# First modulation in five slabs, half of the value products in three one-pass products, scale and shift on ScalarE

## The reference, cut to what matters

```python
mod = cond @ w_ada[l] + b_ada[l]                       # cond = silu(c): one row times a 2048 x 6144 matrix
shift, scale, gate = jnp.split(mod, 3, axis=-1)
h = rms_norm(x, norm_g[l]) * (1.0 + scale[:, None, :]) + shift[:, None, :]
z = h @ w_in[l]
u_a, v_a, g_a, q_b, k_b, v_b, g_b, f_b = jnp.split(z, pts, axis=-1)
```

## Time and profile before

| | |
|---|---|
| median of 3 runs | 2876.5 us (2872.1 to 2881.73) |
| the profiled execution, its time | 2872.35 us |
| its span, first to last instruction | 2870.5 us |
| mean granted TensorE clock | 0.995 |
| busy: TensorE matmuls, VectorE, ScalarE, GpSimd | 2784.9, 1790.2, 1044.7, 43.1 us |
| value stage, first to last value product | 54.05 to about 170.7 us |
| f group, first to last product | 170.66 to about 182.05 us |
| DMA share and rate, 100 to 125 us | 1.00, 350 GB/s |

### The profile page before, as it was taken

The page is one execution under the profiler, slowest core; times in us unless marked ns, Lnnn a source line. Parts: engine busy times, 40 slices in busy tenths (PEclk is TensorE's granted clock), DMA queues, the critical chain, the costliest instruction groups (busy, mean ns, idle before and its releaser), DMA issues.

```text
span 2870.5 us, 35410 instructions
## 1 busy us (share of the span) xinstructions
PE 2784.9 (97%) x12484; PEld 2204.4 (77%) x12484; DVE 1790.2 (62%) x2750; ACT 1044.7 (36%) x1632; POOL 43.1 (2%) x51
## 2 busy tenths in 40 slices
PE   7999999999999989999999999999999999999999
PEld 4468887777788866888877777787778688888887
DVE  6856675555598768445565747383977777525454
ACT  3032222444332365422243534433322542224233
POOL 0000000000000000000000000000000000100000
PEclk9999999999999999999999999999999999999999
DMA  9966553222356647466522223224667265333332
GB/s 353 353 212 214 190 190 96 74 76 79 126 192 219 231 145 244 149 216 197 185 82 83 82 86 103 73 88 139 216 231 220 90 234 192 108 97 96 124 111 96
DMA packets 239243, 451.32 MB, mean 157 GB/s; under 512 B 23919, under 2 KB 45889, under 8 KB 234483
## 3 DMA queue, kind: packets, MB, share of 16 engines
q1 hardware_dynamic: 236288, 440.85, 46.8%
q0 software_dynamic: 2304, 8.39, 0.8%
q10 hardware_dynamic: 504, 0.17, 0.0%
HBM read 422.06 MB, written 27.30 MB: 157 GB/s over the span
## 4 chain that ended last, share of the span: by engine, by line
PE 85%; DVE 5%; ACT 2%; issue 2%; DVEq 2%; DMA 2%; ACTq 1%; SPq 1%
PE ps L1405 20%; PE ps L1411 20%; PE ps L1408 20%; PE ps L1695 4%; PE ps L1424 2%; PE ps L1418 2%; PE ps L1421 2%; PE ps L1936 2%; PE ps L1853 1%; PE ps L1844 1%; PE ps L1375 1%; PE ps L1970 1%; PE ps L1967 1%; PE ps L1380 1%; PE ps L1377 1%
## 5 line engine op out<-in xcount | busy, mean ns | idle before, releaser
L1993 DVE TENSOR_TENSOR w_lo<-w_raw,w_hi 128x512 fp32r<-128x512 f32 (+2 forms) x672 | 448.3, 673 | 542.2 <-ACT w_hi L714 297.8
L1405 PE MATMUL ps<-op_hi,w_hi 128*128 128x512 f32 (+2 forms) x2800 | 779.2, 397 | 6.5 <-ACT w_hi L714 4.5
L1411 PE MATMUL ps<-op_hi,w_lo 128*128 128x512 f32 (+2 forms) x2800 | 754.7, 389 | 5.2 <-DVE w_lo L1993 5.2
L1408 PE MATMUL ps<-op_lo,w_hi 128*128 128x512 f32 (+2 forms) x2800 | 754.9, 389 | 0.6 <-DVE op_lo L2130 0.6
L1411 PEld LDWEIGHTS ps<-op_hi,w_lo 128*128 128x128 f32 (+1 forms) x2800 | 524.8, 188 | 117.8 <-DVE w_lo L1993 7.1
L1408 PEld LDWEIGHTS ps<-op_lo,w_hi 128*128 128x128 f32 (+1 forms) x2800 | 526.1, 188 | 112.8 <-DVE op_lo L2130 1.4
L1405 PEld LDWEIGHTS ps<-op_hi,w_hi 128*128 128x128 f32 (+1 forms) x2800 | 517.4, 188 | 121.8 <-issue 10.3
L714 ACT ACTIVATE w_hi<-w_raw 128x512 fp32r<-128x512 f32 (+2 forms) x416 | 242.7, 592 | 596.0 <-PE ps L1411 437.2
L739 ACT ACTIVATE w_hi<-w_raw 128x512 fp32r<-128x512 f32 x288 | 181.8, 632 | 583.7 <-PE ps L1411 454.2
L2016 DVE SCALAR_TENSOR_TENSOR acc<-a_raw,vec,acc 128x512 f32<-128x512 f32 x525 | 382.1, 747 | 17.5 <-DMA a_raw<-in_w_ada 14.8
L2758 DVE TENSOR_TENSOR w_lo<-w_raw,w_hi 128x512 fp32r<-128x512 f32 x128 | 83.6, 686 | 60.7 <-ACT w_hi L1262 55.2
(11 more groups left out here) (314 smaller groups left out, 2459.3 us busy)
## 6 DMA issues: line engine op xcount, KB each, us to landing
a_raw<-in_w_ada SPq DMA_DIRECT2D x216, 512.0 KB, 4.0
w_raw<-in_w_in_e SPq DMA_DIRECT2D x160, 512.0 KB, 4.7
w_raw<-in_w_in SPq DMA_DIRECT2D x96, 512.0 KB, 4.8
arena<-in_w_ada SPq DMA_DIRECT2D x72, 512.0 KB, 6.7
w_raw<-in_w_in_o SPq DMA_DIRECT2D x64, 512.0 KB, 4.3
w_raw<-in_w_out SPq DMA_DIRECT2D x32, 512.0 KB, 4.9
w_raw<-in_w_out_e SPq DMA_DIRECT2D x32, 512.0 KB, 5.2
w_raw<-in_w_out_o SPq DMA_DIRECT2D x32, 512.0 KB, 3.8
```

The source lines that it names most:

```text
L1405: mm(ps[0:m, bank + j, 0:tok], hi[:, cols], B.op_hi[:, k, 0:tok], start=first, stop=False)
L1408: mm(ps[0:m, bank + j, 0:tok], hi[:, j * P:j * P + m], B.op_lo[:, k, 0:tok], start=False, stop=False)
L1411: last = mm(ps[0:m, bank + j, 0:tok], lo[:, j * P:j * P + m], B.op_hi[:, k, 0:tok], start=False, stop=last_t)
L1993: V.tensor_tensor(B.w_lo[:, c % RING, 0:width], B.w_raw[:, c // 2 % RAW, c % 2, 0:width], B.w_hi[:, c % RING, 0:width].bitcast(f32), ALU.s ...
```

## The change

- The first modulation is made in 5 slabs of 4, 4, 4, 2, 2 tiles. The last two have loads of 256 KB and accumulates of 128x512, 16 each; the norm is 128x1024, the sums are 4 products.
- Scale and shift move from VectorE to ScalarE (`ACT.Identity` with scale and bias). In slabs 0 and 1 the four tiles are modulated and then rounded. From slab 2 (`SPLIT_SLAB`) on ScalarE makes `op_hi` straight from the normed tile, drains, and then modulates the tile in place.
- The value products of slabs 2, 3 and 4 (blocks 8 to 15, 64 of the 128 products) become three fp32r products each. Their 16 weight tiles are split: `w_hi` by ScalarE (`value_high`; the first four ahead of slab 2, those of slabs 3 and 4 behind the slab's tiles), `w_lo` by GpSimd (`value_low`, one 128x512 `tensor_tensor` each), between its loads.
- In slabs 2 to 4 the order within a block is tile by tile; ahead of them, in blocks that are odd, stand the two tiles' products of bank 7. The sums of slabs 3 and 4 are placed behind these, so 18 one-pass products are behind the sums.
- VectorE has the low parts from accumulate 3 on, the norm ahead of park, and the last slab's low parts, its park and the first f weights' low parts between the 16 part accumulates.
- The store of x moves from SyncE's to ScalarE's queue, the load of b_s behind f's weights. The weights of f wait for `lo_done`. The two buffers of the slabs are exchanged.

```diff
-START_RING, SLABS, SLAB = 6, 4, 4
+START_RING, SLABS = 6, 5
+SLAB_AT, SLAB_TILES = (0, 4, 8, 12, 14), (4, 4, 4, 2, 2)
+SPLIT_SLAB = 2
...
+def value_low(B, pool, b):
+    for c in (2 * (b - SPLIT_BLOCK), 2 * (b - SPLIT_BLOCK) + 1):
+        pool.wait_ge(B.sem("hi_done"), c + 1)
+        if c >= RING:
+            pool.wait_ge(B.sem("w_used"), c - RING + 1)
+        B.nc.gpsimd.tensor_tensor(B.w_lo[:, c % RING, :], B.w_raw[:, b % RAW, c % 2, :],
+                                  B.w_hi[:, c % RING, :].bitcast(mybir.dt.float32), mybir.AluOpType.subtract)
+        B.nc.gpsimd.drain().then_inc(B.sem("lo_done"), 1)
...
+        if b >= SPLIT_BLOCK + RAW:
+            value_low(B, pool, b - RAW)
         pool.dma_start(B.w_raw[:, b % RAW, :, :],
...
     for slab in range(SLABS):
+        split = 2 * (SLAB_AT[slab] - SPLIT_BLOCK)
+        if slab == SPLIT_SLAB:
+            for c in range(RING):
+                value_high(c)
+        act.wait_ge(sem("columns_or_parked"), 2 * slab + 1)
+        for t in range(SLAB_TILES[slab]):
+            k = SLAB_AT[slab] + t
+            x, scale, bias = slab_input(B, slab)[:, t, :], B.mod[:, 16 + k:17 + k], B.mod[:, k:k + 1]
+            if slab >= SPLIT_SLAB:
+                Act(B.op_hi[:, k, :], x, ACT.Identity, scale=scale, bias=bias).then_inc(sem("op_high"), 1)
+                nc.scalar.drain()
+            Act(x, x, ACT.Identity, scale=scale, bias=bias).then_inc(sem("modulated"), 1)
+        if slab < SPLIT_SLAB:
...
+        else:
+            for c in range(max(split, RING), split + 2 * SLAB_TILES[slab]):
+                value_high(c)
...
+    def split_products(slab, b, k, blocks):
...
+        for j in blocks:
+            mm(bank, B.op_hi[:, t, rows(j)], hi, start=first, stop=False)
+        pe.wait_ge(sem("lo_done"), c + 1)
+        for j in blocks:
+            mm(value_bank(slab, g, t, j)[0], B.op_hi[:, t, rows(j)], lo, start=False, stop=False)
+        pe.wait_ge(sem("op_tile"), t + 1)
+        for j in blocks:
+            done = mm(bank, B.op_lo[:, t, rows(j)], hi, start=False, stop=last)
...
+                if b == final:
                     last.then_inc(sem("park_summed"), 1)
+                    if slab >= SPLIT_SLAB and slab < SLABS - 1:
+                        reduce_slab(slab + 1)
...
             if kt == 1:
                 slab_columns(slab - 1)
-                slab_modulated(slab - 1)
-            if kt in (4, 5, 6, 7):
-                slab_low(slab - 1, kt - 4)
+            if 3 <= kt < 3 + SLAB_TILES[slab - 1]:
+                slab_low(slab - 1, kt - 3)
             if kt == 15:
+                slab_normed(slab)
                 park(slab - 1)
-                slab_normed(slab)
     slab_columns(SLABS - 1)
-    slab_modulated(SLABS - 1)
-    for t in range(SLAB):
-        slab_low(SLABS - 1, t)
     for t in range(KT):
         part_tile(FIRST["f"], t)
-    park(SLABS - 1)
+        if t < SLAB_TILES[SLABS - 1]:
+            slab_low(SLABS - 1, t)
+        if t == 9:
+            park(SLABS - 1)
+        if t in (9, 11):
+            if t == 9:
+                dve.wait_ge(sem("lo_done"), KT)
+            low_tile(KT + (t - 9) // 2, GROUPS[FIRST["f"]]["width"])
```

More of the change, by code:

```diff
@@ L618, in pool_program @@
             .then_inc(B.va_in[b % RAW], 16)
+    for b in range(KT - RAW, KT):
+        value_low(B, pool, b)
     queries = at(AT_QST, 2, S)
@@ L1683, in reduce_slab @@
         if slab:
-            pe.wait_ge(sem("parked"), slab)
+            pe.wait_ge(sem("columns_or_parked"), 2 * slab)
         else:
             pe.wait_ge(sem("variance"), 1)
-        reduce_parts(slab % 2, ps[:, 7, :]).then_inc(sem("start_summed"), 1)
+        tiles = SLAB_TILES[slab]
+        for v in range(2):
+            for j in range(tiles):
+                last = mm(ps[:, 7, tiles * v + j:tiles * v + j + 1], B.acc[:, slab % 2, v, j * P:(j + 1) * P],
+                          B.ones[:, 0:1], start=True, stop=True)
@@ L1689, in value_product, with value_bank @@
+        last.then_inc(sem("start_summed"), 1)
+    def value_bank(slab, g, t, j):
+        own = g == 1 and j == 3
+        first, last = (SLAB_AT[slab], SLAB_AT[slab] + SLAB_TILES[slab] - 1) if own else (0, KT - 1)
+        return ps[:, 4 * g + j, :], t == first, t == last
     def value_product(slab, b, k, j):
-        g, kt = va_block(b)
+        g, kt = VA_BLOCKS[b]
+        t = kt + k
         pe.wait_ge(B.va_in[b % RAW], 16 * (b // RAW + 1))
-        t = kt + k
-        own = g == 1 and j == 3
@@ L1695, in value_product @@
-        return mm(ps[:, 4 * g + j, :], slab_input(B, slab)[:, t % SLAB, j * P:(j + 1) * P],
-                  B.w_raw[:, b % RAW, k, :], start=t % SLAB == 0 if own else t == 0,
-                  stop=t % SLAB == SLAB - 1 if own else t == KT - 1)
+        pe.wait_ge(sem("modulated"), t + 1)
+        bank, first, last = value_bank(slab, g, t, j)
+        return mm(bank, slab_input(B, slab)[:, t - SLAB_AT[slab], j * P:(j + 1) * P],
+                  B.w_raw[:, b % RAW, k, :], start=first, stop=last)
@@ new lines, in split_products @@
+    def split_products(slab, b, k, blocks):
+        g, kt = VA_BLOCKS[b]
+        t, c = kt + k, 2 * (b - SPLIT_BLOCK) + k
+        hi, lo = B.w_hi[:, c % RING, :], B.w_lo[:, c % RING, :]
+        rows = lambda j: slice(j * P, (j + 1) * P)
+        pe.wait_ge(sem("hi_done"), c + 1)
+        pe.wait_ge(sem("op_high"), t + 1)
+        for j in blocks:
+            bank, first, last = value_bank(slab, g, t, j)
+            mm(bank, B.op_hi[:, t, rows(j)], hi, start=first, stop=False)
[4 more added lines that the diff above has]
+        for j in blocks:
+            bank, first, last = value_bank(slab, g, t, j)
+            done = mm(bank, B.op_lo[:, t, rows(j)], hi, start=False, stop=last)
+        return done
@@ L2452, in slab_low @@
     def slab_low(slab, t):
-        k = SLAB * slab + t
+        k = SLAB_AT[slab] + t
         dve.wait_ge(sem("op_high"), k + 1)
@@ L2516, in vector_program @@
     y_tile = lambda t: Y[:, t, :]
-    for c in range(4):
+    for c in (KT + 2, KT + 3):
         low_tile(c, GROUPS[FIRST["f"]]["width"])
```

141 lines of the change are left out of this document (77 added, 64 removed).

## The result

| | before | after |
|---|---|---|
| median, us (executions) | 2874.86 (4) | 2903.89 (4) |
| lowest to highest | 2872.1 to 2881.73 | 2899.93 to 2908.33 |
| profiled execution / its span | 2872.35 / 2870.5 | 2903.88 / 2902.1 |
| mean granted clock in it | 0.995 | 0.987 |
| f's first product / q's first product, us | 170.66 / 184.02 | 192.12 / 208.07 |

The ratio is 1.0091 (95% interval 1.0077 to 1.0106). The two medians lie 29 us apart, more than twice what was forecast and outside its range; the ratio alone makes it 26 us. At q's first product the delay in the profiled executions is 24.05 us.

A forecast was written before the change was run, and what follows sets the result against it. TensorE was taken as the bound, barely, with VectorE close behind. VectorE's and GpSimd's delays gave +11 us at f's end, clock +1.7, queues +0.6: taken as +13 on 2876.5, so 2889.5 us; range 2869 to 2900.

The forecast's parts named there:

- The store of x takes a turn in ScalarE's queue (0.45 us), beside TensorE: Queue term: the moved store of x costs ScalarE's queue 0.45 us, beside TensorE's work.
- plus 0.15 to signal: Low weight tiles on GpSimd: signalling each finished subtraction adds 0.15 us to its 1.25.
- GpSimd's 1.25 us: Split value products: one 128x512 subtraction on GpSimd takes 1.25 us, a quarter of a longer instruction and a start.
- The exclusion, accumulates too: Slabs 2 to 4: each of 16 GpSimd subtractions takes 1.25 us from VectorE, holding its accumulates; bounds 0 and 1.25.
- TensorE's −10.7: Value products: if only TensorE counted, 64 split products save 11.6 us, less 0.9 for another set of sums.
- The wait of 8 us ahead of slab 4's sums: TensorE reaches slab 4's sums near 152.4 us, VectorE at 160.5, so TensorE waits 8 us.
- The clock, +1.7: Slow clock behind TensorE's gaps: hidden at 134 and 152 us, counted in the f group, +1.7 us.
- q keeps its distance to f's end: q group: its weights follow f's low tile 10, so its start shifts along with f's end.
- A: Rival: accumulates not held by GpSimd, value stage ends near 167.7 us, total 2874.5 us; chance 0.15.
- D: Rival: halved loads with 1 KB rows move fewer bytes, VectorE waits for loads, +3 us more; within chance 0.15 shared with C.
- C: Rival: GpSimd's subtractions take 1.5 to 1.9 us, adding 4 to some 10 us, 2893 to 2900; chance 0.15.
- B: Rival: TensorE stays the bound and the full -10.7 us returns, 2866 us, likelier end 2868; chance 0.05.

The follow-up runs named there:

- e_late: The changed kernel with the store of x moved on ScalarE's queue behind the evacuation of f's bank: 2894.69 us, ratio 1.0068 to the kernel before.
- e_late_nodrain: e_late with GpSimd's drain behind each subtraction removed, the subtraction signalling by itself: 2886.56 us, ratio 1.0035 to the kernel before.
- e_late_memset: e_late_nodrain with GpSimd's subtraction replaced by four memsets of 128x128: 2878.34 us, ratio 1.0007 to the kernel before.
- e_last_only: The changed kernel with late store, low weight parts on VectorE, slabs of 4, 4, 4, 4 tiles, only the last split: 2873.87 us, ratio 0.9991.
- e_last_again: The same kernel as e_last_only, run again in another set: 2873.92 us, ratio 0.9991 to the kernel before.
- e_whole: The changed kernel with late store, low weight parts on VectorE, slabs of 4, 4, 4, 4 tiles, the last two split: 2880.29 us, ratio 1.001.
- e_memset: The changed kernel with GpSimd's subtraction replaced by two memsets with a drain between: 2904.23 us (one execution).

## Why the prediction was wrong

The direction was right and the size was not: +13 forecast, +29 measured by the medians and +26 by the ratio. The delay of q's first product (24.05 us in the profiles) falls in three steps of known cause, which the experiments take away one behind the other:

| taken away | kernel | q's first product, less by | between the marks, less by | ratio, less by |
|---|---|---|---|---|
| the store's place | e_late | 7.2 us | 5.6 us | 0.0023 (6.6 us) |
| the drains | e_late_nodrain | 7.1 us | 7.0 us | 0.0033 (9.5 us) |
| GpSimd's reading beside VectorE | e_late_memset | 9.6 us | 11.5 us | 0.0028 (8.1 us) |

What is left is within 0.3 us of the kernel before at both marks, and 0.0007 by the ratio, whose interval takes in 1. The three views of a step differ by 1.6 to 3.4 us, which is how well its size is known. Only the third was in the sum.

- **The step that failed first** was "The store of x takes a turn in ScalarE's queue (0.45 us), beside TensorE". It costed the issue (0.36 us in the profile) and not the 4 MB behind it, while it did cost the bytes of b_s, an eighth as many. Nor did it ask when the store would now be issued: at 173.12 instead of 149.85. The landing of f's first weights became 9.9 us in the middle, and the Gelu that stands behind them on ScalarE kept TensorE from f for 8.17 us. With the store elsewhere this hole is gone, and the time is 6 to 9 us less.
- **The second** was GpSimd's "plus 0.15 to signal". The term was a drain behind a load in flight. Four of them took 4.0 to 5.6 us. "Waits some 2.5 us for the first low tiles" became 5.18, and slab 3's sums came at 144.1 instead of 139. Without the drains TensorE's waits for GpSimd fall from 7.0 to 1.6 us.
- **GpSimd's 1.25 us**: right, 1.27 at the shortest, up to 1.59 in the kernel after.
- **The exclusion, accumulates too**: right. e_late_nodrain is the kernel that the sum described. Its VectorE takes from columns (110.41) to the end of the park (136.92) 26.5 us; the sum had 16.3 + 8 x 1.25 = 26.3. Its f starts at 177.08, against 177.8 in the sum; TensorE waits there for VectorE's low tile until 181.33, with 183.2 in the sum; its last f product begins at 191.89, against an end of 193. This execution was ahead by 2 us already at slab 2's columns (110.41, against 112.4 in the sum); from there to f's end it takes 81.7 us, and the sum had 80.6. Its time is 9.3 us over the kernel before, where the sum said 13. The Trainium skill (SBUF — State Buffer, "SBUF: two separate sides") has this exclusion for VectorE instructions with two SBUF inputs beside a reading GpSimd; the runs agree: 1.34 us per accumulate over a stretch with subtractions beside it, 0.84 with memsets beside it.
- **TensorE's −10.7**: the rates were right (four products in 0.91 us), and where VectorE and ScalarE could follow they paid: counted from slab 2's sums, f's first product comes 4.8 us earlier in e_last_only and 4.7 in e_last_again, where 32 split products at the sum's 0.18 us give 5.8.
- **The wait of 8 us ahead of slab 4's sums**: 6.45, for the reason named.
- **The clock, +1.7**: right in kind, and in part in the wrong place. The sum held the slow stretch behind the gap ahead of slab 4's sums to be hidden, with ScalarE and GpSimd setting the end of the value stage. In e_late_nodrain TensorE runs there without a wait from 158.40 to 177.08, with a granted clock of 0.50 up to 163 us, so the slow stretch counts in full; GpSimd's last subtraction is over at 171.1, early enough. That the sum's 177.8 came out so close is luck in this step. In e_whole the same effect stood ahead of twice as many tiles.
- **q keeps its distance to f's end**: right, about 2 us in both kernels.
- **Rivals.** A gave 2874.5, 2 us under the kernel before; with the holding taken away, and with it the drains and the store's place (e_late_memset), the time was 0.3 us over it. So A's mechanism is absent from this chip's traces and its price was nearly right. Its marks came true up to slab 4's sums: slab 3's sums began at 134.78 us and its park was over at 151.68, against 134.3 and 151.4 in A; the 2 us behind them, f at 169.95 against a value stage that ends near 167.7, are the granted clock of 0.50 from 151.8 to 156 us, which A had left out. D's waits for loads were 4.1 us there and cost little. C fell with the 1.27 us. B fell too: TensorE was not the bound.

What stays open: from q's first product to the end the profiled executions took between 2686.5 us (before) and 2696.1 (e_memset), 2694.0 in the kernel after and 2694.1 in e_last_only. These differences follow no change that was made, and were not traced. The kernel before alone varies by as much: 2872.28 us, with a mean granted clock of 0.995, to 2882.38, with 0.992. So a single profiled span says nothing about a few microseconds, and the 2 to 5 us that 26 or 29 us leave over the 24.05 at q are not shown to belong to the change. Which part of the last-slab kernel's 4 us belongs to the late store was not run by itself.

## What to carry to other kernels

When a transfer is moved, cost its bytes where it lands in time, not its issue: ask which small loads are queued beside it in those microseconds, and what stands behind the instruction that waits for them. Before work goes to an idle engine, ask what that engine already does in its queue (loads in flight, drains) and which engine its reads will hold; here VectorE did the 16 tiles more cheaply itself. A faster form pays only in the stretch where the other engines have room: split the last slab, where VectorE had 6.95 us to spare, and not the ones where it had none. This wait stands in VectorE's timeline of the kernel before, ahead of its last park:

```profile
166.11 0.69 DVE L2466 TENSOR_TENSOR arena<-arena,ps 128x512 f32<-128x512 f32 x1 [6.95 <-PE ps L1695]
```

When single profiles are compared, count from a mark that lies ahead of all that the edit touches: here the executions were up to 2.7 us apart before the changed part began.

## What the runs showed of the hardware that was not expected

A drain on GpSimd waits for the load that GpSimd has issued: 5.58 us behind a landing of 5.5, 4.60 behind 4.5, 10.67 behind 10.7, and 1.35 to 1.66 with nothing in flight. A signal on the computing instruction itself does not wait so: TensorE's waits for GpSimd were 1.6 us instead of 7.0. A load of 112 KB that lands in 2.2 us in a quiet stretch takes 8.4 to 11.3 us beside a 4 MB store on another queue, and 15.3 us behind it on the same queue. GpSimd's memsets beside VectorE's accumulates don't lengthen them (0.85 us each), its subtractions do; two of these with nothing between them hold one accumulate for both (3.2 to 3.8 us instead of 0.75). And in the same stretch of the same instructions, 54 to 57 us, the granted clock was 1.00 in some executions and 0.50 to 0.70 in others.
